# Mixture-of-experts block on one core: tokens picked for four experts at once from split rows, and expert outputs added to the residual by one-hot products

## Chip, cores and metric

One NeuronCore of a Trainium2 chip runs the whole two-layer block as one program. The metric is the device time of one execution in microseconds (us); lower is better. Engines are named as in the profile: PE (TensorE, matmuls), PEld (its weight loads), DVE (VectorE), ACT (ScalarE), POOL (GpSimd), SP (SyncE, which here only issues DMAs). PSUM is the memory that PE writes, 8 banks of 512 fp32 columns.

## What is computed

```
for layer in range(2):
    ...                                   # norm, three token mixers, merge, gated residual
    h  = modulate(rms_norm(x), ...)                       # (T, 1024), T = 512 in layer 0, 256 in layer 1
    g, top2 = route(h)                                    # one of 4 groups, two of its 8 experts
    w  = p_group * softmax over the two                   # (T, 2)
    for e in range(32):                                   # one SwiGLU expert, D 1024, width 512
        y_e = (silu(h @ w_gate[e]) * (h @ w_up[e])) @ w_down[e]
    x += gate * sum over the token's two experts of w * y_e
out = rms_norm(x[latent]) * g
```

Everything is fp32. Layer 0 carries 256 latent and 256 context tokens, layer 1 only the 256 latent ones. An expert's weights are 4.19 MB (gate and up) and 2.10 MB (down), so each layer streams 32 x 6.29 = 201.3 MB through its expert loop.

## The kernel before

The residual `xt` is kept transposed in SBUF: 8 chunks of 128 channels by 512 tokens. Each engine runs its own instruction stream, written by hand; semaphores order them. A layer is: norm, the mixers (PE products of weights that SP streams through the three slots of `ws`), merge and output product, second norm, routing, expert loop, combination.

**Split products.** In the mixers a product of fp32 matrices is made of three products of type fp32r: ACT rounds each operand to a high part, DVE leaves the low part (`round_weights`, `leave_weights`), and PE runs hi x hi, hi x lo, lo x hi (`product`, L457 to L459). The expert products (L709, L721), the picks (L700) and the transposes are plain fp32.

**Routing.** After the logits PE turns `ht` into token rows `hr` (4 tiles of 128 tokens by 1024), ACT copies them. DVE finds each token's two experts, its position within each (`place1`), the count `n_of` and the first row `start_of` of every expert in a sorted list, `dest` (the row of each token's output in that list) and the two weights `route_w`.

**Expert loop** (`Fori(0, 16)`, two experts per pass, slots s = 0, 1). Per expert PE runs: `gate_up` (8 chunks k by two halves j of the output width, the 64 token slots as stationary operand, 512 columns moving, the halves in the two 64-column halves of the array); the first half of `pick_x` for the next expert (one-hot product of `hr` with `pick`, 8 chunks by nt token tiles, 64 columns moving; nt is 4 in layer 0 and 2 in layer 1); `turn_h`; the second half of the pick; `down` (4 k by 2 halves). ACT does the silu, copies the 64 output rows out of PSUM and stores them to the DRAM tensor `y_rows` (`save_rows`). DVE multiplies silu by up (L1415), copies the turned rows (L1433) and the picked tokens (L1435) and sets the next `pick` (L1378). An expert with more than 64 tokens repeats the whole for its next 64 inside an `If` (the overflow block).

**Weights.** SP loads experts e and e+1 into two slots; gate/up of e+2 waits for `turn_h` of e, down of e+2 for `down` of e:

```
sp.wait_ge(g["hidt_done"].sem, NE * l + 2 * i + slot - 1)
load_expert(source, slot, range(4))
sp.wait_ge(down_done[slot].sem, 16 * l + i)
load_expert(source, slot, range(4, 6))
```

**Combination**, after the loop: ACT waits until every row store has landed; POOL gathers the two rows of each token by indirect DMA (L1545), ACT and DVE weight and add them (L1080, L1449), PE turns the tile back (L783), DVE adds it to `xt` (L1443), ACT squares (L1073), PE averages the squares (L773), and ACT's root (L839) opens the next norm.

## Time and profile before

| | |
|---|---|
| median of 3 runs | 2273.63 us (2273.55 to 2279.94) |
| the profiled execution | 2275.08 us |
| its span | 2273.3 us |
| PE busy | 2084.5 us, 92% |
| DVE / ACT / POOL busy | 647.3 / 514.7 / 155.0 us |
| mean granted PE clock | 0.956 of full speed |

The span is the time from the first to the last record of one execution, the time of the execution has 1.8 us more around it. Places in the program are given as us from the start of the span: expert loop of layer 0 from 667 to 1289, of layer 1 from 1717 to 2234.

### The profile page before, as it was taken

Reading aid. Unit: us, or ns where it says so; the run is one execution under the profiler, and the core shown is the slowest. Engines: PE = TensorE matmul, PEld = TensorE weight load, DVE = VectorE, ACT = ScalarE, POOL = GpSimd, SP = SyncE. Lnnn points to the kernel's source line nnn. Section 1 sums busy time; section 2 is a strip of 40 time slices with the busy share of each in tenths; the row PEclk is TensorE's granted clock in tenths of the full one; section 3 lists DMA queues with packets and bytes.
Section 4 is the critical chain, followed back from the end, with each engine's and each line's share of the span. In section 5 each row is a group of like instructions: output and inputs, shape, how many; then the busy total and the mean of one; then the engine's idle time right before and its main releaser. Section 6 shows DMA issues by size and latency. Waiting matters only on the chain.

```text
span 2273.3 us, 31445 instructions
## 1 busy us (share of the span) xinstructions
PE 2084.5 (92%) x11703; PEld 1329.6 (58%) x11704; DVE 647.3 (28%) x1392; ACT 514.7 (23%) x1028; POOL 155.0 (7%) x190
## 2 busy tenths in 40 slices
PE   5899999999979999999999769988988999999995
PEld 2666666678746555656566457766765444444443
DVE  1554354345341100101011166373341111111112
ACT  2444333432220000100000154343131001111111
POOL 0043030000000000000000105040000000000000
PEclk8899999999979999999999889988998999999997
DMA  6266565123258998956888424232458679999992
GB/s 216 96 222 190 199 204 185 52 74 95 73 223 359 367 366 365 367 209 257 340 351 358 177 67 122 60 115 66 139 196 345 284 323 421 420 421 420 421 421 108
DMA packets 95915, 551.01 MB, mean 242 GB/s; under 512 B 14034, under 2 KB 15010, under 8 KB 42596
## 3 DMA queue, kind: packets, MB, share of 16 engines
q1 hardware_dynamic: 83108, 526.89, 59.5%
q0 software_dynamic: 4224, 11.35, 1.8%
q10 hardware_dynamic: 8512, 11.81, 1.5%
q8 instruction: 47, 0.77, 0.1%
q14 instruction: 24, 0.20, 0.0%
HBM read 537.15 MB, written 12.85 MB: 242 GB/s over the span
## 4 chain that ended last, share of the span: by engine, by line
PE 75%; DMA 10%; DVE 6%; ACT 5%; issue 2%; SPq 1%; ACTq 0%; POOL 0%; DVEq 0%; POOLq 0%
PE ps L709 19%; PE ps L700 15%; PE ps L721 9%; PE ps L457 7%; PE ps L459 7%; PE ps L458 7%; DMA moe<-in_w_exp_gate_up_dram 6%; PE ps L575 3%; DMA ws<-in_w_in_dram 2%; PE ps L604 2%; PE ps L586 1%; PE ps L497 1%; ACT w_hi L856 1%; DVE w_lo L1132 1%; PE ps L715 1%
## 5 line engine op out<-in xcount | busy, mean ns | idle before, releaser
L709 PE MATMUL ps<-moe,arena 128*64 128x512 f32 x2176 | 486.9, 600 | 10.6 <-DMA moe<-in_w_exp_gate_up_dram 5.6
L700 PEld LDWEIGHTS ps<-arena 128*128 128x128 f32 x3360 | 395.9, 196 | 58.3 <-issue 54.2
L700 PE MATMUL ps<-arena 128*128 128x64 f32 x3360 | 407.3, 279 | 5.9 <-DVE arena L1383 4.4
L709 PEld LDWEIGHTS ps<-moe,arena 128*64 128x64 f32 x2176 | 159.3, 139 | 325.8 <-issue 311.8
L457 PE MATMUL ps<-ht_hi,w_hi 128*128 128x512 f32 (+1 forms) x736 | 268.4, 365 | 26.6 <-DVE ht_lo L1155 17.9
L458 PE MATMUL ps<-ht_lo,w_hi 128*128 128x512 f32 (+1 forms) x736 | 257.7, 350 | 0.0
L459 PE MATMUL ps<-ht_hi,w_lo 128*128 128x512 f32 (+1 forms) x736 | 257.6, 350 | 0.0
L721 PE MATMUL ps<-moe,arena 128*64 128x512 f32 x1088 | 248.5, 598 | 2.1 <-DVE arena L1427 2.1
L1132 DVE TENSOR_TENSOR w_lo<-ws,w_hi 128x1024 fp32r<-128x1024 f32 (+1 forms) x124 | 152.5, 1233 | 288.4 <-ACT w_hi L856 288.3
L1415 DVE TENSOR_TENSOR arena<-aux,ps 128x256 f32<-128x256 f32 x64 | 27.0, 422 | 686.3 <-ACT aux L1030 686.3
L457 PEld LDWEIGHTS ps<-ht_hi,w_hi 128*128 128x128 f32 x736 | 140.0, 190 | 79.9 <-issue 50.0
L856 ACT ACTIVATE w_hi<-ws 128x1024 fp32r<-128x1024 f32 (+1 forms) x124 | 127.5, 1028 | 244.4 <-PE ps L459 129.9
L1053 ACT ACTIVATE arena<-ps 128x512 f32<-128x512 f32 x64 | 38.2, 597 | 529.8 <-PE ps L721 529.8
L459 PEld LDWEIGHTS ps<-ht_hi,w_lo 128*128 128x128 f32 x736 | 140.3, 191 | 18.5
L458 PEld LDWEIGHTS ps<-ht_lo,w_hi 128*128 128x128 f32 x736 | 140.7, 191 | 15.6
L721 PEld LDWEIGHTS ps<-moe,arena 128*64 128x64 f32 x1088 | 72.0, 136 | 123.8 <-issue 116.5
L1545 POOL DMA_INDIRECT arena<-y_rows,dest x12 | 11.6, 966 | 1658.2 <-ACTq L1065 947.9
L1030 ACT ACT_TABLE_LOAD x32 | 41.1, 1283 | 241.7 <-PE ps L709 241.7
L575 PE MATMUL ps<-arena 64*128 64x512 f32 (+1 forms) x192 | 87.5, 579 | 0.0
L1435 DVE COPY arena<-ps 128x512 f32<-128x512 f32 x64 | 44.3, 692 | 140.9 <-PE ps L700 140.9
L1030 ACT ACTIVATE aux<-ps 128x256 f32<-128x256 f32 x64 | 24.6, 384 | 201.0 <-PE ps L709 200.6
L586 PE MATMUL ps<-ident,moe 128*128 128x128 f32 x320 | 47.3, 290 | 18.5 <-DVE moe L1250 18.3
(207 smaller groups left out, 1844.1 us busy)
## 6 DMA issues: line engine op xcount, KB each, us to landing
moe<-in_w_exp_gate_up_dram SPq DMA_DIRECT2D x256, 1024.0 KB, 10.6
moe<-in_w_exp_down_dram SPq DMA_DIRECT2D x128, 1024.0 KB, 11.7
moe<-in_w_mod_dram SPq DMA_DIRECT2D x32, 1536.0 KB, 7.8
ws<-in_w_in_dram SPq DMA_DIRECT2D x92, 512.0 KB, 3.5
y_rows<-arena ACTq DMA_DIRECT2D x164, 64.0 KB, 5.7
ws<-in_w_branch_dram SPq DMA_DIRECT2D x16, 512.0 KB, 3.6
ws<-in_w_out_dram SPq DMA_DIRECT2D x16, 512.0 KB, 3.4
aux<-in_rpb_a_dram POOLq DMA_DIRECT2D x64, 64.0 KB, 2.7
```

The costliest lines, as they stand in the source:

```text
L457: pe.matmul(ps[:, bank, 0:cols], w[:, k, :], a_hi, start=(i == 0), stop=False)
L458: pe.matmul(ps[:, bank, 0:cols], w[:, k, :], a_lo, start=False, stop=False)
L459: mm = pe.matmul(ps[:, bank, 0:cols], w_lo[:, slot, k, :], a_hi, start=False, stop=(k == rows[-1]))
L575: mm = pe.matmul(score_bank[:, qt, 0:n], q_of(kind)[rows, h // 2, q0 + qt * P:q0 + (qt + 1) * P], kt_of(kind, h)[:, keys], start=True, sto ...
L586: mm = pe.transpose(prob_bank[:, tile, qt * P:(qt + 1) * P], prob[h % 2][:, qt, tile * P:(tile + 1) * P], ident[:, :])
L604: mm = pe.matmul(pv_bank[HD * hh:HD * hh + HD, 0:SEQ], v_of(kind, 2 * pair + hh, tile + (4 - n)), prob_t[hh][:, tile, :], start=(tile == 0 ...
L700: mm = pe.matmul(ps[:, dst_bank, c * BLK:(c + 1) * BLK], hr[:, tile, c * P:(c + 1) * P], picks[:, tile, :], start=(tile == 0), stop=(tile ...
L709: mm = pe.matmul(ps[BLK * j:BLK * j + BLK, bank, :].rearrange("p (g n) -> p g n", g=2), xs[:, k, :], w[:, k, 512 * j:512 * j + 512].rearra ...
L721: mm = pe.matmul(ps[BLK * j:BLK * j + BLK, bank, :], src[:, k % 2, BLK * (k // 2):BLK * (k // 2) + BLK], w[:, k, 512 * j:512 * j + 512], s ...
L856: nc.scalar.activation(w_hi[:, i % 2, 0:m], ws[:, slot, 0:m, :], ACT.Copy) \
L1030: nc.scalar.activation(act_g[s], ps[:, 2 + s, 0:256], ACT.Silu).then_inc(g["silu_done"].sem, 1)
L1132: v.tensor_tensor(w_lo[:, ws_slots[item], 0:m], ws[:, ws_slots[item], 0:m, :], w_hi[:, i % 2, 0:m].bitcast(F32), ALU.subtract).then_inc(g[ ...
```

## The change

* `hr` is held as `hr_hi` and `hr_lo` (both fp32r, ACT and DVE). `pick4` is a one-hot matrix for four experts, so a pick product moves 256 columns, not 64; it runs twice, for high and low rows. Each expert's pass does a quarter of the next four experts' picks (two of eight channel chunks), and ACT copies them into one of two buffers `xg`.
* The output rows of an expert stay in SBUF, scaled by the slots' routing weights `wsl` and split into `y_hi` (ACT) and `y_lo` (DVE). The pick matrix `pick_b` (bf16, twice side by side so that both halves of 64 rows hold it) is turned by PE into `spread_b` (slots by tokens), and three bf16 parts of the weights give `wsl`. Once per pair of experts, inside the first expert's `gate_up`, four rounds of eight products y x spread (64 rows deep, the two output halves in the array's two row halves) put 8 chunks into banks 3, 5, 7, and DVE adds them to `xt`.
* Gone: `y_rows`, `start_of`, `dest`, the row stores, the gathers, the weighting and turning after the loop. In their place stand one last combination and the ordinary `squares`/`mean`.
* The loop body now holds eight experts: `Fori(0, 3)` and a written-out last pass. All experts use bank 2 for gate/up and bank 4 for down. The overflow block picks from split rows, and ends with its own four combination rounds.
* `y_hi`, `y_lo`, `spread_b` lie in the memory of `ws`, so SP waits for the last combination before it loads layer 1's first mixer weights. POOL clears them once per layer.
* Routing: DVE makes `hr_lo` (`low_rows`) ahead of the positions.

```diff
@@ SP
-                        sp.wait_ge(g["hidt_done"].sem, NE * l + 2 * i + slot - 1)
+                        sp.wait_ge(g["slots_done"].sem, NE * l + 2 * i + slot - 1)
                         load_expert(source, slot, range(4))
...
+                sp.wait_ge(g["comb_done"].sem, 4 * EVENTS * (l + 1))
@@ PE
-                def pick_x(dst_bank, picks, sem, chunks=range(KC)):
-
-                    for c in chunks:
-                        for tile in range(nt):
-                            mm = pe.matmul(ps[:, dst_bank, c * BLK:(c + 1) * BLK], hr[:, tile, c * P:(c + 1) * P], picks[:, tile, :],
-                                           start=(tile == 0), stop=(tile == nt - 1))
...
+                def pick_chunk(bank, half, c, picks, n):
+
+                    for tile in range(nt):
+                        for rows in (hr_hi, hr_lo):
+                            mm = pe.matmul(ps[:, bank, n * half:n * half + n], rows[:, tile, c * P:(c + 1) * P], picks[:, tile, :],
+                                           start=(tile == 0 and rows is hr_hi), stop=(tile == nt - 1 and rows is hr_lo))
...
+                def combine(bank_done, done, ready, slots, event=None):
+
+                    def turn(rnd):
+                        banks = [COMBINE_BANKS[(2 * rnd + j) % 3] for j in range(2)]
+                        if rnd == 0:
+                            ready()
+                        pe.wait_ge(bank_done.sem, event + max(0, 2 * rnd - 1) + 1)
+                        terms = [(part[s], s) for s in slots for part in (y_hi, y_lo)]
+                        for n, (y, s) in enumerate(terms):
+                            for j in range(2):
+                                half = slice(BLK * j, BLK * j + BLK)
+                                mm = pe.matmul(ps[:, banks[j], 0:w_all], y[half, rnd * P:(rnd + 1) * P], spread_b[s][half, 0:w_all],
+                                               start=(n == 0), stop=(n == len(terms) - 1))
+                        mm.then_inc(done.sem, 1)
...
+                        if between and k in (2, 4, 6, 7):
+                            between((2, 4, 6, 7).index(k))
...
+                def turn_slots(picks, weights, sem):
+
+                    for tile in range(nt):
+                        pe.matmul(ps[:, 6, tile * P:(tile + 1) * P], picks[:, tile, :], ident_b[:, :], start=True, stop=True)
+                    for tile in range(nt):
+                        mm = pe.matmul(ps[:, 1, 256:259], picks[:, tile, :], weights[:, tile, :], start=(tile == 0), stop=(tile == nt - 1))
@@ ACT
-                        act.wait_ge(y_copied[s].sem, mine + 2)
-                        act.wait_ge(g["yo_saved"].sem, act.snap(n_more, min_val=0, max_val=64) * 32 + 32)
-                        save_rows(ysb[s], row, y_saved[s], rows=HALF)
...
+                        act.wait_ge(g["slots_done"].sem, own + 1)
+                        nc.scalar.activation(spread_b[s][:, 0:w_all], ps[:, 6, 0:w_all], ACT.Copy).then_inc(g["slots_copied"].sem, 1)
...
+                        nc.scalar.activation(y_hi[s][:, :], ps[:, 4, :], ACT.Copy, scale=wsl[:, s:s + 1]).then_inc(g["y_hi_set"].sem, 1)
@@ DVE
+                def add_round(rnd, done, signal, at):
+                    dve.wait_ge(done.sem, at + rnd + 1)
+                    for j in range(2):
+                        c = 4 * j + rnd
+                        for st, cols in streams(l):
+                            ins = v.scalar_tensor_tensor(xt[:, c, cols], ps[:, COMBINE_BANKS[(2 * rnd + j) % 3], cols],
+                                                         modv[:, l, st, 5 * KC + c:5 * KC + c + 1], xt[:, c, cols], ALU.mult, ALU.add)
+                        ins.then_inc(signal.sem, 1)
+
+                def leave_y(s, scale, signal):
+                    v.scalar_tensor_tensor(y_lo[s][:, :], ps[:, 4, :], scale, y_hi[s][:, :].bitcast(F32), ALU.mult, ALU.subtract).then_inc(signal.sem, 1)
@@ POOL
-                        pool.indirect_dma_start(out=yg[tile % 2][k], out_offset=None, in_=y_rows[0:2 * w_all, :],
-                                                in_offset=bass.IndirectOffsetOnAxis(ap=dest[:, k, tile:tile + 1], axis=0)) \
```

**How the order of instructions moves.** First PE, the end of an even expert's pass in layer 0 before (`arena` holds rows, picks and hidden rows, `moe` the weights): the turned rows, the second half of the pick, `down`, then the next expert's `gate_up` and the first half of its pick.

```order
L715 MATMUL ps<-ident,arena 128x128 [waits hid_done0]
L715 MATMUL ps<-ident,arena 128x128
L700 MATMUL ps<-arena 128x64 x16
L721 MATMUL ps<-moe,arena 64x512 [waits y_copied0,hidt_copied]
L721 MATMUL ps<-moe,arena 64x512 x7
L709 MATMUL ps<-moe,arena 64x512 [waits gu_in1,xt_copied]
L709 MATMUL ps<-moe,arena 64x512 x15
```

The same place now, from the last quarter of the even expert's `gate_up` (L735) on: a combination round (L725) stands after it, and the loop's branch comes before the picks (L710, here four of eight rows) and the turned slots (L745, L747).

```order
L735 MATMUL ps<-moe,xg_57 64x512 x2
L725 MATMUL ps<-spread_b_59,y_hi_61 128x512 [waits comb_added]
L725 MATMUL ps<-spread_b_59,y_hi_61 128x512
L725 MATMUL ps<-spread_b_59,y_lo_63 128x512 x2
L725 MATMUL ps<-spread_b_60,y_hi_62 128x512 x2
L725 MATMUL ps<-spread_b_60,y_lo_64 128x512 x2
L710 MATMUL ps<-pick_55,hr_hi 128x256 [waits pick4_set]
L710 MATMUL ps<-pick_55,hr_lo 128x256
L745 MATMUL ps<-ident_b,arena 128x128 [waits wsl_set,pickb_set]
L747 MATMUL ps<-mrow,arena 128x3 x4
L752 MATMUL ps<-ident,arena 128x128 [waits hid_done]
L758 MATMUL ps<-moe,arena 64x512 [waits hidt_copied]
```

Per expert 32 pick products of 64 columns became 16 of 256, and each pair of experts got 32 combination products. Second DVE, an even expert of layer 0: three rounds of additions to `xt` (L1469) stand ahead of the silu product (L1484), and one behind it, ahead of the copy of the turned rows.

```order
L1469 SCALAR_TENSOR_TENSOR xt<-ps,modv,xt 128x256 [waits comb_done]
L1469 SCALAR_TENSOR_TENSOR xt<-ps,modv,xt 128x256 x3
L1465 REGISTER_ALU
L1484 TENSOR_TENSOR arena<-aux,ps 128x256 [waits silu_done]
L1469 SCALAR_TENSOR_TENSOR xt<-ps,modv,xt 128x256 [waits comb_done]
L1469 SCALAR_TENSOR_TENSOR xt<-ps,modv,xt 128x256 x3
```

Where DVE had only the silu product (L1415) before the copy of the turned rows (L1433), it now has 16 additions of 256 columns around it.

## Rows read from the trace of the kernel before

**Rows 1.** Page, the chain that ended last, shares by engine.

```profile
PE 75%; DMA 10%; DVE 6%; ACT 5%; issue 2%; SPq 1%; ACTq 0%; POOL 0%; DVEq 0%; POOLq 0%
```

**Rows 2.** Stretches (us, busy and instructions by engine, clock, DMA share, GB/s): both loops.

```profile
680.00:966.00 286.00, 286.00 (x1821) 171.44 (x1820) 29.93 (x64) 25.97 (x40) 0.00 (x0) 1.00 0.89 362
...
2036.00:2219.50 183.50, 176.09 (x986) 88.11 (x984) 20.83 (x48) 19.48 (x31) 0.00 (x0) 1.00 1.01 421
```

**Rows 3.** The chain (start, us, what), layer 0 loop, one expert.

```profile
687.88 6.87 PE ps L709 x32
694.75 3.72 PE ps L700 x32
698.46 0.23 PE ps L715 x2
698.69 3.52 PE ps L700 x32
702.21 3.58 PE ps L721 x16
```

**Rows 4.** The chain, layer 1 loop, DMA-bound stretch.

```profile
2036.33 7.09 PE ps L709 x32
...
2047.31 19.42 DMA moe<-in_w_exp_gate_up_dram
...
2066.87 3.19 PE ps L709 x13
```

**Rows 5.** Timeline of PE, fp32r products in layer 1's mixers and output product.

```profile
1347.16 0.39 PE L458 MATMUL ps<-ht_lo,w_hi 128*128 128x512 f32 x1
1347.39 0.40 PE L459 MATMUL ps<-ht_hi,w_lo 128*128 128x512 f32 x1
...
1684.85 0.28 PE L458 MATMUL ps<-mt_lo,w_hi 128*128 128x256 f32 x1
1684.97 0.28 PE L459 MATMUL ps<-mt_hi,w_lo 128*128 128x256 f32 x1
```

**Rows 6.** Groups by line and form (busy, mean ns, idle before).

```profile
L1053 ACT ACTIVATE arena<-ps 128x512 f32<-128x512 f32 x64 | 38.2, 597 | 529.8 <-PE ps L721 529.8
...
L1378 DVE TENSOR_TENSOR arena<-arena,slots 128x256 f32<-128x256 f32 x32 | 13.3, 415 | 0.0
...
L1155 DVE TENSOR_TENSOR ht_lo<-ht,ht_hi 128x512 fp32r<-128x512 f32 x16 | 11.1, 692 | 3.2 <-ACT ht_hi L869 3.1
...
L1301 DVE SCALAR_TENSOR_TENSOR xt<-ps,half_gate,xt 128x256 f32<-128x256 f32 x24 | 10.9, 480 | 30.9 <-PE ps L459 30.9
```

**Rows 7.** Page, DMA issues (count, KB each, us to landing), the row stores.

```profile
y_rows<-arena ACTq DMA_DIRECT2D x164, 64.0 KB, 5.7
```

**Rows 8.** Timeline of PE, layer 0: expert 17's picks, its block's end.

```profile
981.25 10.93 PE L700 MATMUL ps<-arena 128*128 128x64 f32 x96
...
1008.52 0.43 PE L715 MATMUL ps<-ident,arena 128*128 128x128 f32 x2 [1.24 <-issue]
```

**Rows 9.** The chain, layer 1: gate_up of expert 2 and of expert 3.

```profile
1747.99 6.89 PE ps L709 x32
...
1784.01 1.28 PE ps L709 x5
```

**Rows 10.** Timeline from layer 0's last product to the root.

```profile
1285.29 3.65 PE L721 MATMUL ps<-moe,arena 128*64 128x512 f32 x16
...
1325.84 0.69 ACT L839 ACTIVATE aux<-ps,eps 128x512 f32<-128x512 f32 x1 [2.19 <-PE ps L773]
```

**Rows 11.** Timeline, the same in layer 1.

```profile
2230.46 3.65 PE L721 MATMUL ps<-moe,arena 128*64 128x512 f32 x16
...
2260.31 0.47 ACT L839 ACTIVATE aux<-ps,eps 128x256 f32<-128x256 f32 x1 [3.07 <-PE ps L773]
```

**Rows 12.** Timeline, start of layer 0's loop.

```profile
652.68 13.92 PE L700 MATMUL ps<-arena 128*128 128x64 f32 x64 [2.23 <-DVE arena L1383]
...
667.46 2.83 PE L709 MATMUL ps<-moe,arena 128*64 128x512 f32 x6 [0.87 <-DVE arena L1410]
```

More of the change, by code:

```diff
@@ L789, in _ @@
-                for bank in (2, 3, 4, 5):
-                    claim(bank)
-                mean_tile(nt - 1)
-                free[6] = (g["rstd_sqrt"], after)
+                        more_units = not (last and q >= 4)
+                        if more_units:
+                            if q % 4 == 0:
+                                pe.wait_ge(g["pick4_set"].sem, 8 * l + 2 * i + q // 4 + 2)
+                            pick_chunk(0, 0, 2 * (q % 4), pick4, 4 * BLK)
+                        pe.wait_ge(g["pickb_set"].sem, own + 1)
@@ L793, in _ @@
+                for c in COMBINED:
+                    mean(*after, c)
+            pe.wait_ge(g["comb_added"].sem, 8 * EVENTS * DEPTH + 1)
             for tile in range(2):
@@ L825, in squares @@
                     act.wait_ge(g["prep"].sem, g["prep"].at("xt", KC - 1))
-                for c in range(KC):
+                order = chunk_order(l, which)
+                for at, c in enumerate(order):
                     if which == "n2":
@@ L1084, in _ @@
-                square_tile(nt - 1)
-                root(*after, nt - 1)
+                        act.wait_ge(g["slots_done"].sem, own + 1)
+                        nc.scalar.activation(spread_b[s][:, 0:w_all], ps[:, 6, 0:w_all], ACT.Copy).then_inc(g["slots_copied"].sem, 1)
+                        if not (last and q >= 4):
+                            act.wait_ge(g["unit_done"].sem, own + 5)
+                            nc.scalar.activation(xg[(q // 4 + 1) % 2][:, 2 * (q % 4):2 * (q % 4) + 2, :],
+                                                 ps[:, 0, :].rearrange("p (c n) -> p c n", c=2), ACT.Copy).then_inc(g["unit_copied"].sem, 1)
@@ L1394, in _ @@
+                set_pick4(0)
+                for n in range(6, 2 * nt):
+                    low_rows(n)
                 dve.wait_ge(g["r_exp_done"].sem, g["r_exp_done"].at(l, 1))
@@ new lines, in eight_experts @@
+                        if not (last and q == 7):
+                            if q == 7:
+                                set_weights(e + 1)
+                            set_pick(pick_b, e + 1, 0, g["pickb_set"])
+                        if q % 4 == 3 and not last:
+                            dve.wait_ge(g["unit_done"].sem, own + 5)
+                            set_pick4(e + 5)
+                        dve.wait_ge(g["y_hi_set"].sem, own + 1)
+                        leave_y(s, wsl[:, s:s + 1], g["y_lo_set"])
@@ L1455, in _ @@
+                with dve.Fori(0, 3) as i:
+                    eight_experts(i, False)
+                eight_experts(3, True)
+                for rnd in range(4):
+                    add_round(rnd, g["comb_done"], g["comb_added"], 4 * EVENTS * l + 64)
             reciprocal_rms(DEPTH - 1, "fin")
```

440 lines of the change are left out of this document (223 added, 217 removed).

## Prediction

> **What bounds the kernel now.** I first read the chain that ended last: PE carries 75% of it, DMA 10% [rows 1]. The table of stretches then splits the two expert loops, which are half of the run. In layer 0 PE is busy for all of 286 us at full clock while the DMA engines stand at 0.89 of their time and 362 GB/s; in layer 1 DMA is at 1.01 and 421 GB/s, which is its ceiling here [rows 2]. So the first loop is bound by PE, the second by the stream of expert weights.
>
> The chain shows the parts of one expert in layer 0: gate/up 6.87 us, half a pick 3.72, the turn 0.23, the other half 3.52, down 3.58, together 17.92 [rows 3]. The picks are 7.2 of these. In layer 1, with two token tiles instead of four, they are half as long, so PE needs 14.3; but two experts take 2066.87 - 2036.33 = 30.54 us, 15.27 each, and a 19.4 us transfer stands in the chain between them [rows 4]. After each loop comes a stretch with little PE work: from the end of the last down product to the root of the next norm 1325.84 - 1288.94 = 36.9 us in layer 0 [rows 10] and 2260.31 - 2234.11 = 26.2 us in layer 1 [rows 11].
>
> **The change, layer 0 loop, per pair of experts.** Before: 2 x 17.92 = 35.8 us. Now:
> - gate/up and down as before, 2 x (6.87 + 3.58) = 20.9, turns 0.5 [rows 3].
> - Picks: 16 products of 256 columns per expert, fp32r. Neighbouring fp32r products of 256 columns start 0.118 us apart, those of 512 columns 0.23 [rows 5]. 2 x 16 x 0.118 = 3.8, in place of 14.5.
> - Turned slots and slot weights: 8 small bf16 products per expert, no row has their form. They stream 4 x 128 and 4 x 3 columns; between 0.2 (the column rate of rows 5) and 0.9 (each priced as a 256-column product) I take 0.4, nearer the first because columns are few: 0.8 per pair.
> - Combination: 32 products of 512 columns. No row shows two products in different row halves side by side. The two column halves of gate/up do run side by side: 16 fp32 products take 6.87, that is 8 times 0.86, and 0.86 is four passes of 0.215 [rows 3]. I take the same for row halves: 16 x 0.23 = 3.7; the other end is 7.4.
> - Eight changes between array layouts. Down is 3.58 where half of gate/up is 3.43, so a change shows as 0.15 [rows 3]; 8 x 0.15 = 1.2. The Trainium skill (TensorEngine Tiling, Key Properties) says that a change of tiling mode drains the engine, which speaks against this interleaving. A product of 512 columns lasts 0.39 us though the next starts 0.23 behind it [rows 5], so a drain would show about 0.16, and the row agrees.
> - Waits. The rounds use banks 3, 5, 7 in turn, so round 1 waits for one of DVE's additions, 2 for three, 3 for five. An addition to a chunk is two instructions of 0.48 [rows 6], so about 1.0 per chunk, and a gate/up step between rounds is 0.86, twice where two steps stand between. The first two waits are covered. Behind round 3 the queue is tight: on DVE the silu product stands behind three rounds of additions and the copy of the turned rows behind the fourth, 1.9 us. I put 0.4 there, and 0.3 for the branch, which PE now meets right behind gate/up. Bounds 0 and 3.
>
> Sum 31.3, 15.7 per expert; 4.5 us per pair saved, 16 pairs: -72. The last four experts carry no picks (4 x 1.9): -8. I give 4 back for what the expert at the head of each eight may wait (table load, copies of picks): -76.
>
> ACT and DVE stay hidden in this loop: per pair DVE has 7.7 us of additions, 1.4 of low parts (0.69 each [rows 6]) and some 6 of copies and one-hots, 15 of 31; if PE did not cover them, the bound would still be PE.
>
> **Overflow blocks.** Two in layer 0, two in layer 1. One costs 1008.52 - 984.9 = 23.6 us now, where 984.9 is a third of the way into the 96 pick instructions [rows 8]; in layer 1 expert 2 takes 36.02 instead of 14.3, 21.7 more [rows 9]. The block gains: outputs scaled and split (0.60 + 0.69 + hand-overs, 1.45), then four rounds with nothing to run beside the additions: 16 x 0.48 = 7.7 in layer 0, 3.8 in layer 1, and 1 for the rounds. The picks there keep 64 columns; 64 fp32r products, between 0.03 each (a quarter of the 256-column product) and 0.114 (today's picks, 10.93 / 96 [rows 8]); I take no gain. With the later start +11 each in layer 0, +7 in layer 1: +22 and +14.
>
> **Start of the loops.** DVE makes the low rows ahead of the one-hots: six of 0.69 and four one-hots of 0.42 [rows 6] before PE's first pick, two more low rows before it may start. PE's prologue of 64 products is between 7.6 (full clock) and 14 (half clock), today 13.9 and then a copy [rows 12]: +4 in layer 0, +2 in layer 1.
>
> **Layer 1 loop.** PE would need 20.9 + 0.5 + 1.9 + 0.4 + 1.9 + 1.2 + 0.7 = 27.5 per pair, 13.7 per expert, below the weights' 15.27. The row stores leave the DMA engines: two of 64 KB per expert [rows 7], 0.13 MB beside 6.29. At the same 421 GB/s an expert costs 6.29 / 6.42 x 15.27 = 14.96; over 30 experts -9. The longer blocks hold both weight slots, so DMA idles for what they add. Sum: -9 + 14 + 2 = +7.
>
> **Behind the loops.** Now: split (1.45), four rounds and the additions, squares and means chunk by chunk behind them. A mean is one fp32 product of 512 columns, 0.86 at full and 1.7 at half clock; eight of them at half clock are 13.7 and set the pace. From down to root 16 in layer 0 and, at half the width, 9.5 in layer 1: -21 and -17. Layer 1's first mixer weights now start behind the last round; three loads of under 4 us each lie beside the additions, the means and the root: nothing, and at most 4 if that cover is gone. The removed sort on DVE was off the path.
>
> **Sum:** -76 + 22 + 4 + 7 - 21 - 17 = -81, from 2275.08 for the profiled execution to 2194. The median of the runs shown lies 1.5 below that execution: **2193 us**.
>
> **The rivals.**
> A, the forecast, 0.64: layer 0 bound by PE at some 15.7, layer 1 by DMA. Its own range is 2165 to 2225.
> B, the row halves run one after the other, 0.10. For it: no row shows them together, and they read and write different places than the column halves. Against: the column halves do overlap. Price 3.7 x 16 = 59 in layer 0 and some 5 in layer 1: 2257. The Trainium skill (TensorE: Matmul & The Clock Gate, Part 3) measures four row tiles at 3.07 times one, so not full overlap; carried over to two halves that estimate adds 18 us to the sum.
> C, slower than before, 0.06: rounds and additions alternate. If each round can start only when DVE has finished the one before, and DVE does nothing while PE computes, every even expert stands for 4 x 1.92 = 7.7 us in layer 0 and 3.8 in layer 1. That is +7 x 16 = 112 and, as layer 1 then passes the weights' pace, about +25: 2330. It decides from 81 / 16 = 5.1 us of waiting per pair on. Against it: three banks, and 1.7 us of gate/up between most rounds.
> D, layer 0 becomes DMA-bound too, 0.16: small waits vanish, 15.0 per expert (-22), and the blocks' picks run at their columns' rate (-15): 2156.
> E, layout changes cost more than 0.15, 0.04: at the 0.39 us that a whole product lasts [rows 5], eight of them cost 1.9 more per pair, +31 in layer 0: 2224. This is the drain of the Trainium skill's page named above (TensorEngine Tiling) at its worst.
>
> **How the numbers follow.** What this kernel's measurement tells from no change is 0.3%, 6.8 us, so faster means below 2266.8. A, D, E and most of B lie there: 0.64 + 0.16 + 0.04 + 0.07 = 0.91. Same is B's rest, 0.03. Slower is C, 0.06. The range 2148 to 2240 leaves out B's and C's middle and the edges of A and D.
>
> **What would show it.** Layer 0's loop near 568 us instead of 621.5, picks as 256-column products 0.12 apart, the two products of a combination step starting together, PE idle under 1 us in an even expert. In layer 1 15.0 us per expert with DMA still full. From the last down to the root about 16 and 9.5 us. I am wrong if combination products of a step start 0.2 us apart (B), if PE's waits are on DVE's `xt` (C), or if DMA waits appear in layer 0 (D).

## The result, and the profile after

The changed kernel takes 2298.72 us (median of 4 runs, 2292.02 to 2305.78) against 2273.59 for the kernel before (median of 4 runs too; the table above has the first three): 1.0105 times as long, interval 1.0075 to 1.0136. The forecast was 2193 us, in a range of 2148 to 2240. It is slower, by 25 us, and the forecast is off by 106. The profiled execution is the one of 2305.78 us, 30.6 us longer in span than that of before; the rows below are from it.

The page of the changed kernel first: the lines that answer to [rows 1], with the instruction queue, which the forecast did not weigh.

```profile
q8 instruction: 156, 2.56, 0.5%
...
PE 73%; DMA 9%; DVE 7%; issue 5%; ACT 5%; SPq 1%; DVEq 0%; ACTq 0%
```

The row stores are gone, and "issue" has grown from 2% to 5% of the chain: time in which TensorE waits for nothing that the profile shows. The queue that brings instructions moved 156 packets of 16 KB. In the kernel before it is this line:

```profile
q8 instruction: 47, 0.77, 0.1%
```

Next the table of stretches of the changed kernel (columns as in [rows 2]): layer 0's loop from its first gate/up to its last down, nearly two undisturbed pairs of experts within it, layer 1's loop, and in it the DMA-bound part.

```profile
667.33:1320.28 652.95, 575.52 (x3092) 267.15 (x3092) 204.69 (x490) 76.56 (x132) 0.00 (x0) 0.93 0.72 291
...
687.20:750.00 62.80, 61.90 (x359) 28.07 (x356) 23.53 (x56) 9.08 (x16) 0.00 (x0) 1.00 0.96 392
...
1734.53:2277.56 543.03, 490.55 (x2668) 203.86 (x2668) 134.78 (x332) 69.28 (x132) 0.00 (x0) 0.96 0.86 352
...
2003.00:2249.00 246.00, 225.35 (x1234) 90.22 (x1232) 62.17 (x153) 33.64 (x64) 0.00 (x0) 0.98 1.01 416
```

The same stretch of the kernel before:

```profile
667.46:1288.94 621.48, 614.41 (x3876) 366.28 (x3876) 63.78 (x136) 53.30 (x83) 0.00 (x0) 0.99 0.78 317
```

The two kernels enter this loop at the same moment. Within 687 to 750 us the new one does what was forecast: PE busy, full clock, and the weights run at 392 GB/s. Over the whole loop its PE is idle for 77 us where the old one's was for 7, the clock stands at 0.93, and DMA at 0.72. Less work, in more time.

The chain of the changed kernel for an undisturbed pair of experts in layer 0, the answer to [rows 3] (start, us, what):

```profile
687.20 6.87 PE ps L735 x32
694.07 1.14 PE ps L710 x8
695.21 0.24 PE ps L745 x4
695.45 0.08 PE ps L747 x4
...
696.76 3.58 PE ps L758 x16
700.35 2.58 PE ps L735 x12
702.92 1.12 PE ps L725 x7
704.04 1.87 PE ps L735 x8
705.91 1.12 PE ps L725 x8
...
712.20 0.46 issue
...
719.01 3.00 PE ps L735 x13
```

From 687.20 to 719.01 are 31.81 us for two experts, where 31.3 was forecast and 35.8 stood before. L710 are the wide picks, 1.14 + 0.95 = 2.1 us per expert in place of 7.2. A round of combination (L725) is 1.12 us for eight products of 512 columns; that is four pairs side by side, 0.92 at 0.23 each, and the change of layout ahead of them. The `gate_up` with its four rounds takes 12.0 us in all (700.18 to 712.20), where 6.87 and 3.7 leave 1.5 for the eight layout changes, 0.18 each; 1.2 was forecast.

Now a loop-back of the same loop, 84 us later. The timeline of PE (start, us, line, what, and in brackets the idle time before it and what ended it):

```profile
799.74 3.65 PE L758 MATMUL ps<-moe,arena 128*64 128x512 f32 x16
806.86 4.49 PE L735 MATMUL ps<-moe,xg 128*64 128x512 f32 x12 [3.47 <-issue]
```

The first three steps of the next gate/up take 4.49 us where the pair above has 2.58. The table of stretches tells why, and the last row of it shows the same in a block's picks (the last three columns are clock, DMA share, GB/s):

```profile
799.80:803.30 3.50, 3.50 (x17) 1.00 (x16) 1.62 (x5) 0.60 (x1) 0.00 (x0) 1.00 0.95 342
803.40:806.80 3.40, 0.00 (x0) 0.00 (x0) 0.75 (x1) 1.97 (x2) 0.00 (x0) 1.00 1.01 419
806.86:811.30 4.44, 4.44 (x14) 1.12 (x14) 0.00 (x0) 0.00 (x0) 0.00 (x0) 0.62 1.01 415
981.70:992.60 10.90, 10.90 (x54) 10.90 (x54) 0.00 (x0) 0.00 (x0) 0.00 (x0) 0.50 0.01 5
```

TensorE stands for 3.47 us with nothing to wait for, then works at a granted clock of 0.62, most of it at the lower level of 1.2 GHz. So a stop of 3.5 us costs 5.4. The weights stream at 419 GB/s throughout, and are not missing. The list of waits (line, releaser: us in all, times, longest) shows how often it happens from 667 to 1320 us:

```profile
PE ps L710 <- issue: 38.0, 20, 6.7
PE ps L745 <- issue: 9.0, 6, 2.7
PE ps L725 <- DVE xt L1469: 7.3, 7, 1.4
PE ps L735 <- issue: 6.4, 2, 3.5
```

In these lines TensorE stands 53 us by issue, with four more in lines not shown, where the kernel before has 2.6 in all. Not all of it has one cause: 17 of the 57 us stand inside or at the end of the two overflow blocks. The wait that rival C feared, on DVE's `xt`, is 7.3, and 5.8 of that stands in the blocks' rounds too.

Last the overflow block of expert 17, timeline of PE, the answer to [rows 8]:

```profile
970.48 7.04 PE L735 MATMUL ps<-moe,xg 128*64 128x512 f32 x32
980.22 0.30 PE L710 MATMUL ps<-pick_o,hr_hi 128*128 128x64 f32 x1 [2.71 <-DVE pick_o L1494]
980.35 0.28 PE L710 MATMUL ps<-pick_o,hr_lo 128*128 128x64 f32 x1
...
992.36 0.40 PE L710 MATMUL ps<-pick_o,hr_lo 128*128 128x64 f32 x1
...
993.54 9.66 PE L735 MATMUL ps<-moe,arena 128*64 128x512 f32 x32 [0.24 <-DVE arena L1496]
...
1010.54 0.50 PE L725 MATMUL ps<-spread_b,y_hi 64*128 64x512 f32 x2 [1.71 <-issue]
```

The 64 picks last 12.4 us: the first dozen stand 0.11 us apart, the rest 0.21, at a clock of 0.50, and gate/up behind them takes 9.66 instead of 7.04. After the fourth round PE stands another 6.64 us until 1024.36. From 977.52, where gate/up ends, that makes 46.8 us; with the half clock behind it, expert 17 lasts some 49 us longer than an expert without a block. Before it was 23.6, and 35 was forecast.

Between the layers the new kernel is faster, as was forecast. From the last down product to the root, the timeline has these rows for layer 0:

```profile
1316.63 3.65 PE L758 MATMUL ps<-moe,arena 128*64 128x512 f32 x16 [0.52 <-DVE arena L1512]
...
1339.38 0.69 ACT L903 ACTIVATE aux<-ps,eps 128x512 f32<-128x512 f32 x1 [0.59 <-PE ps L522]
```

19.1 us, against 36.9 before [rows 10] and 16 forecast. The timeline between them: 1.6 us for the split of the rows, 9.3 for the four rounds, three of which wait 0.97 each for DVE's additions, then 8.1 for the eight means, at a granted clock of 0.87. In layer 1 it is 2277.56 to 2290.98, 13.4, against 26.2 [rows 11] and 9.5. The account of the span: layer 0's loop +31.5, layer 1's +26.0 (543.03 against 517.06), the two stretches behind them -17.8 and -12.8, between root and next loop +3.9, the rest -0.2: +30.6 us. Single executions enter layer 0's loop anywhere from 667 to 678 us in this study, so parts of one or two us mean little.

### The profile page after: what moved, and what is told of

Read it like the earlier page. It is cut to its first block, busy times and chain, and to the rows that moved or that the text cites. A ratio compares the mean times of both kernels' runs of the same rounds, so it can differ in the third digit from the quotient of the medians.

```text
span 2303.9 us, 28909 instructions
## 1 busy us (share of the span) xinstructions
PE 2029.3 (88%) x10751; PEld 1170.4 (51%) x10752; DVE 862.5 (37%) x1919; ACT 554.8 (24%) x1138; POOL 145.5 (6%) x190
## 4 chain that ended last, share of the span: by engine, by line
PE 73%; DMA 9%; DVE 7%; issue 5%; ACT 5%; SPq 1%; DVEq 0%; ACTq 0%
PE ps L735 19%; PE ps L758 8%; PE ps L464 7%; PE ps L466 7%; PE ps L465 7%; PE ps L725 6%; PE ps L710 6%; DMA moe<-in_w_exp_gate_up_dram 6%; PE ps L583 3%; DMA ws<-in_w_in_dram 2%; PE ps L612 2%; PE ps L594 1%; PE ps L522 1%; ACT w_hi L920 1%; PE ps L504 1%
## 5 line engine op out<-in xcount | busy, mean ns | idle before, releaser
L735 PE MATMUL ps<-moe,xg 128*64 128x512 f32 x2048 | 480.7, 606 | 24.5 <-DMA moe<-in_w_exp_gate_up_dram 13.7
L735 PEld LDWEIGHTS ps<-moe,xg 128*64 128x64 f32 x2048 | 138.9, 138 | 292.2 <-issue 268.3
L1469 DVE SCALAR_TENSOR_TENSOR xt<-ps,modv,xt 128x256 f32<-128x256 f32 x456 | 192.6, 478 | 215.3 <-PE ps L725 210.2
L758 PE MATMUL ps<-moe,arena 128*64 128x512 f32 x1088 | 254.6, 609 | 10.5 <-DVE arena L1512 7.1
L710 PE MATMUL ps<-pick,hr_hi 128*128 128x256 f32 x384 | 119.1, 335 | 54.4 <-issue 45.5
L758 PEld LDWEIGHTS ps<-moe,arena 128*64 128x64 f32 x1088 | 73.5, 140 | 144.2 <-issue 122.9
L725 PE MATMUL ps<-spread_b,y_hi 64*128 64x512 f32 (+1 forms) x576 | 114.6, 404 | 25.5 <-DVE xt L1469 15.4
L725 PEld LDWEIGHTS ps<-spread_b,y_hi 64*128 64x128 f32 x576 | 55.8, 190 | 149.5 <-DVE xt L1469 101.6
L710 PEld LDWEIGHTS ps<-pick,hr_hi 128*128 128x128 f32 x384 | 81.7, 213 | 89.1 <-issue 89.1
L710 PE MATMUL ps<-pick,hr_lo 128*128 128x256 f32 x384 | 107.2, 304 | 4.8 <-issue 4.8
L1484 DVE TENSOR_TENSOR arena<-aux,ps 128x256 f32<-128x256 f32 x64 | 26.8, 419 | 193.4 <-ACT aux L1087 193.4
L725 PE MATMUL ps<-spread_b,y_lo 64*128 64x512 f32 (+1 forms) x576 | 98.2, 347 | 0.0
```

The costliest lines, as they stand in the source:

```text
L710: mm = pe.matmul(ps[:, bank, n * half:n * half + n], rows[:, tile, c * P:(c + 1) * P], picks[:, tile, :], start=(tile == 0 and rows is hr_ ...
L725: mm = pe.matmul(ps[:, banks[j], 0:w_all], y[half, rnd * P:(rnd + 1) * P], spread_b[s][half, 0:w_all], start=(n == 0), stop=(n == len(term ...
L735: mm = pe.matmul(ps[BLK * j:BLK * j + BLK, 2, :].rearrange("p (g n) -> p g n", g=2), xs(k), w[:, k, 512 * j:512 * j + 512].rearrange("p (g ...
L758: mm = pe.matmul(ps[BLK * j:BLK * j + BLK, 4, :], src[:, k % 2, BLK * (k // 2):BLK * (k // 2) + BLK], w[:, k, 512 * j:512 * j + 512], star ...
L1469: ins = v.scalar_tensor_tensor(xt[:, c, cols], ps[:, COMBINE_BANKS[(2 * rnd + j) % 3], cols], modv[:, l, st, 5 * KC + c:5 * KC + c + 1], x ...
```

## The experiments

Two theories. **Theory 1**: the loops' bodies have become too long for what TensorE keeps of its code at hand, so it stands at branches and at the loop's end, and comes back at half clock. **Theory 2**: it is the branch, which TensorE now meets directly behind gate/up and its rounds. Beside them stands the work in the blocks, which both kernels have. Each ratio below is to the kernel before as it ran beside that experiment, 2270.7 to 2272.1 us.

**The kernel before, with longer passes.** Nothing is changed but how many experts are written out in one pass of the loop.

```diff
-                with pe.Fori(0, NE // 2) as i:
-                    for s in range(2):
-                        e, done = 2 * i + s, NE * l + 2 * i + s
-                        mine = 16 * l + i
+                with pe.Fori(0, NE // 8) as i:
+                    for q in range(8):
+                        s = q % 2
+                        e, done = 8 * i + q, NE * l + 8 * i + q
+                        mine = 16 * l + 4 * i + q // 2
```

With 16 experts (the same edit, with 16):

> The kernel before with its expert loop written out 16 experts per pass instead of 2, nothing else changed. Theory 1 (the changed kernel's PE stalls, 'issue' of 2 to 7 us, are instruction fetch: its layer 0 pass holds 1420 matmuls, and what lies behind the first four or five experts of a pass must be fetched anew through DMA queues full of weights): this pass holds 1984 matmuls, so the same 2 to 4 us stalls appear in layer 0 although the order of the work is the old one, in 10 to 25 places; time 2273.6 + 25 to 70 us, and several times more bytes on the instruction queue (0.77 MB before). Theory 2 (the stalls come from the branch, which PE now meets directly behind gate/up): no stalls, time within 5 us of before.

Measured: 2304.94 us, 1.0146 times before (1.0102 to 1.0190), 146 packets on the instruction queue. The time is in Theory 1's range, the number of places is not: TensorE stands by issue for over 1.3 us, outside the blocks, in five places of the two layers, not in 10 to 25.

With 8 experts:

> The kernel before with 8 experts per pass: 992 matmuls in a pass of layer 0, about as many as the changed kernel's layer 1 pass (1040), which shows hardly any stall after its first pass. Theory 1: few stalls, 0 to 15 us over before. Theory 2: none, within 5 us.

Measured: 2306.64 us, 1.0153 (1.0104 to 1.0203), 153 packets. An old kernel with the old order of work, only written out further, loses over 30 us, more than the change did, and more than the 0 to 15 that Theory 1 had given it. TensorE stands by issue at each loop-back of layer 0 for 2.65 to 2.91 us, and the gate/up behind takes 8.5 to 8.8 us instead of 7.04. The first of them (timeline):

```profile
822.18 8.62 PE L709 MATMUL ps<-moe,arena 128*64 128x512 f32 x32 [2.65 <-issue]
```

Theory 2 falls as the sole cause.

**The changed kernel, 4 experts per pass.** The picks of the next four experts are gathered in a second buffer and moved over at the end of the pass.

```diff
-                with pe.Fori(0, 3) as i:
-                    eight_experts(i, False)
-                eight_experts(3, True)
+                with pe.Fori(0, 7) as i:
+                    four_experts(i, False)
+                four_experts(7, True)
```

> The changed kernel with a loop of 4 experts per pass (710 matmuls in layer 0): picks for the next four go to one buffer and are moved to the other at the end of a pass (a copy of 1 us each on ACT and DVE beside the down product). Theory 1: the stalls go (58 us in layer 0's loop, 19 in layer 1's) and with them DMA idles less: 2298.7 - 60 to - 80, that is 2220 to 2240 us, faster than before. Theory 2: every branch still stands behind gate/up, stalls stay, 2290 to 2305 us.

Measured: 2280.81 us, 1.0022 (1.0000 to 1.0044), 121 packets. The direction is right and the size missed: the stops inside a pass are gone save for one of 1.1 us and one of 2.7, but those at the loop's end stayed, six of 2.9 to 3.5 us in layer 0, and so did the blocks. The first of them (timeline):

```profile
739.97 4.49 PE L735 MATMUL ps<-moe,xg 128*64 128x512 f32 x12 [3.14 <-issue]
```

**The block taken out, with its code.** The branch stays, with one empty instruction inside (slots past 64 are left out).

```diff
                         with pe.If(n > BLK):
-                            with pe.Fori(1, nb) as b:
-                                ...
+                            pe.nop()
```

> The changed kernel, 8 experts per pass, with the overflow block's work left out of its If (a no-op stands there; tokens beyond the 64th of an expert are dropped), the count's load, the waits and the branch kept at their place: 530 matmuls per pass. Theory 1: no stall, and the four blocks (some 49 us each in layer 0, 31 in layer 1, with stalls) gone too: 2110 to 2150 us. Theory 2: stalls of 2 to 4 us at the branches stay: 2160 to 2200 us.

Measured: 2085.45 us, 0.9180 (0.9141 to 0.9218), 25 us below Theory 1's range, 62 packets, and stalls by issue from 667 to 1300 us of 3.4 us in all, none over 0.5. The block's code and its work together cost 213 us.

**The block's code left in, but never entered** (slots past 64 are left out), which tells the two apart:

```diff
-                        with pe.If(n > BLK):
+                        with pe.If(n > 8 * BLK - 1):
```

> The changed kernel with the overflow block's instructions all in place, but its condition set so that no expert enters it (the outputs of the slots past 64 are left out). The same work as in the kernel whose block has no instructions (2085.45 us), so every difference is the price of code that is only jumped over. Theory 1 (a large loop body is fetched late, and each late fetch also leaves TensorE at half clock behind it): TensorE's stalls by issue outside the blocks were some 50 us in the changed kernel, with as much again in half-clock stretches behind them, so 2140 to 2180 us, stalls at the loop's end and at the branches of experts 5 to 7, and over 130 packets on the instruction queue where the empty block had 62. Rival (the time is the work in the blocks, and code that is not run costs nothing): 2083 to 2095 us.

Measured: 2153.37 us, 0.9502 (0.9475 to 0.9529), and 156 packets. Code that is never run costs 67.9 us. It is that of TensorE, VectorE and ScalarE together; a run further down adds code to TensorE alone. In the profiled executions layer 0's loop takes 554.0 us against 502.5 without the code, layer 1's 485.6 against 474.1. The waits of this kernel from 667 to 1300 us:

```profile
PE ps L710 <- issue: 25.5, 19, 3.6
PE ps L745 <- issue: 8.9, 6, 2.6
PE ps L735 <- issue: 6.0, 2, 3.0
```

**The same of the kernel before.** Its stores must still write every row, so the place of a token is cut to the last slot and the block keeps one store of old rows (slots past 64 are left out).

```diff
-                        with pe.If(n > BLK):
+                        with pe.If(n > 8 * BLK - 1):
...
                     chain(v.tensor_reduce(pos_k[k], wide, AX, ALU.add))
+                    chain(v.tensor_scalar(pos_k[k], pos_k[k], float(BLK - 1), None, ALU.min))
```

> The kernel before, with TensorE, VectorE's and ScalarE's work of its overflow blocks never entered (the slots past 64 are left out: their places are cut to the last slot, and only the store of 64 old rows stays in the block, so that every row is written). Four blocks of 23.7, 23.6, some 20 and 18 us go: 2180 to 2195 us by both theories, since this kernel's loop shows no late fetch. It gives the change without its blocks: my forecast for the rest of the change was -81 minus the blocks' +36, so -117, against 2085.45 us that would be 2202; every us below that is what the forecast of the rest missed.

Measured: 2197.99 us, 0.9669 (0.9639 to 0.9699), 47 packets; 3 us above the expected range, and it holds four stores and their waits that the others have not. With it the 25 us come apart, by the medians. The runs of one kernel here lie 6 to 22 us apart, and by the intervals of the ratios each of the first three differences is good to some 10 us:

| | before | change | difference |
|---|---|---|---|
| the rest of the kernel | 2197.99 | 2085.45 | -112.5 |
| code that is jumped over | - | 67.9 | +67.9 |
| work in the four blocks | 75.6 | 145.4 | +69.8 |
| all | 2273.59 | 2298.72 | +25.1 |

**The block's picks turned round.** The one-hot slots become the stationary operand and the token rows move, 512 columns at a time.

```diff
-                                    for c in range(KC):
-                                        mm = pick_chunk(0, c, c, pick_o, BLK)
+                                    for j in range(2):
+                                        for tile in range(nt):
+                                            for rows in (hr_hi, hr_lo):
+                                                mm = pe.matmul(ps[0:BLK, 2 * j, :], pick_o[:, tile, :], rows[:, tile, 512 * j:512 * j + 512],
+                                                               start=(tile == 0 and rows is hr_hi), stop=(tile == nt - 1 and rows is hr_lo))
+                                        mm.then_inc(g["xro_done"].sem, 1)
+                                    for j in range(2):
+                                        pe.wait_ge(g["xro_copied"].sem, 2 * more + j + 1)
+                                        pe.nop(nofuse=True)
+                                        for c in range(4):
+                                            mm = pe.transpose(ps[:, 0, BLK * (4 * j + c):BLK * (4 * j + c) + BLK],
+                                                              xr_o[j][s][0:BLK, c * P:(c + 1) * P], ident[0:BLK, 0:BLK])
```

With 4 experts per pass:

> The changed kernel with 4 experts per pass, and in the block the picks turned round: the one-hot slots are the 64-column stationary operand and the token rows move, 512 columns each, so 16 products in layer 0 (8 in layer 1) in place of 64 (32) products of 64 columns, then two copies and 8 transposes of 64x128. Price: 16 x 0.23 = 3.7, a copy some 0.9, transposes some 1.2 and a wait, 6 to 7.5 us in place of 13.3 to 13.8 in layer 0, and 4.5 to 5.5 in place of 5.2 at full clock in layer 1. The block's code is also 42 products shorter. Theory 1: -13 from the picks and -5 to -15 from less code to fetch on 2280.81, so 2253 to 2263 us, which would be below the kernel before. Rival (what is saved on TensorE is lost in waits for VectorE's copies, or the block's end stall stays): 2268 to 2282 us.

Measured: 2212.86 us, 0.9735 (0.9709 to 0.9761), 63 packets. 40 us better than the best that was expected. Layer 0, the same block (timeline of PE):

```profile
948.61 0.45 PE L805 MATMUL ps<-hr_hi,pick_o 128*64 128x512 f32 x1 [2.70 <-DVE pick_o L1515]
...
954.59 7.09 PE L736 MATMUL ps<-moe,arena 128*64 128x512 f32 x32 [0.38 <-DVE arena L1520]
...
969.00 0.49 PE L726 MATMUL ps<-spread_b,y_hi 64*128 64x512 f32 x2 [1.71 <-issue]
...
982.83 0.57 PE L711 MATMUL ps<-pick,hr_hi 128*128 128x256 f32 x1 [6.60 <-issue]
```

From the first pick to gate/up 5.98 us in place of 13.3, and gate/up has full clock behind the same wait of 2.7: the granted clock is 1.00 over the wide picks and over gate/up, where it was 0.50 and 0.73. No stall at the loop's end is left, and the packets have fallen from 121 to 63: some 76 instructions less per expert brought the pass below a limit, which is placed further down.

With 8 experts per pass, as in the change:

> The same block with 8 experts per pass as in the changed kernel. Theory 1: -13 from the picks of layer 0 and -10 to -20 from less code to fetch per pass, which is longer here than with 4 experts: 2265 to 2276 us against 2298.72. Rival (code that is jumped over costs nothing): 2283 to 2287 us.

Measured: 2256.37 us, 0.9928 (0.9901 to 0.9956), 143 packets, so 42.4 below the changed kernel and 9 below the range of Theory 1. With 8 experts the pass is still too long, so these 42 are what the picks, their clock and a shorter jump give; with 4 experts they give 68, and the 26 more fit the loop's end: six stops and the slower gate/up behind each are gone.

**The block's inner loop ended after the blocks that there are.** It made 7 turns in layer 0 and 3 in layer 1, of which all but one found nothing to do (the lines below are TensorE's; the loops of the two other engines are changed alike).

```diff
-                            with pe.Fori(1, nb) as b:
-                                with pe.If(n > b * BLK):
+                            blocks = pe.snap((n + BLK - 1) >> 6, min_val=2, max_val=nb)
+                            with pe.Fori(1, blocks) as b:
```

> The kernel with 4 experts per pass and wide picks (2212.86 us), and the block's inner loop ending after the blocks that an expert has, in place of 7 turns (3 in layer 1) of which all but one find nothing to do. In that kernel TensorE stands still by issue for 6.60 and 6.71 us at the end of layer 0's blocks (7 turns, 6 of them empty) and 2.84 and 2.83 in layer 1's (3 turns, 2 empty): a line through both gives 0.95 us per empty turn. Theory 3 (the empty turns are the price, not a fetch): 2 x 5.7 + 2 x 1.9 = 15 us less, 2196 to 2202 us, the stalls near 1 us. Rival (it is the code behind the block that is fetched late): the stalls stay, 2210 to 2216 us.

Measured: 2207.40 us, 0.9693 (0.9664 to 0.9722). This is the fastest kernel of the study; the intervals of the two ratios overlap, so its lead over the one before it is likely, not sure. The stall at the end of the block:

```profile
983.50 0.57 PE L711 MATMUL ps<-pick,hr_hi 128*128 128x256 f32 x1 [2.11 <-DVE xt L1490]
```

It is now 2.11 us and ended by DVE's additions, where it was 6.60 and by issue; in layer 1 it went from 2.83 to 1.33. Six empty turns gone in layer 0 and two in layer 1 give the same 0.75 us each. So the empty turns were the price at this place, and I had first read those 6.6 us as a late fetch. The expectation forgot that the additions stand behind them: 4.5 and 1.5 us per block come free, 12 in all, not 15, and the medians show 5.5.

**The kernel before with 4 experts per pass**, to place the limit:

> The kernel before with 4 experts written out in a pass in place of 2; 8 and 16 had cost +34 and +32 us. TensorE's instructions in a pass of layer 0 (each product is two, its load and itself): 500 before, 1991 with 8, and 997 here. The passes that showed no late fetch have 500, 1143 and 1231, those that showed it 1543 and more. Theory 1 with a limit between 1231 and 1543: no difference, 2268 to 2278 us, and some 50 packets on the instruction queue. Rival (the loss grows with the pass's length from the start): +10 to +17, so 2282 to 2290 us.

Measured: 2302.43 us, 1.0137 (1.0100 to 1.0175), 116 packets. Both ranges are missed. The chain of this kernel and of the kernel before, at the same place:

```profile
739.66 3.00 PE ps L721 x14
742.67 2.69 issue
745.36 8.49 PE ps L709 x32
```

```profile
741.61 6.87 PE ps L709 x32
748.48 3.72 PE ps L700 x32
```

The new one stands at each of layer 0's seven loop-backs for 2.7 to 2.9 us, and nowhere in layer 1. What was wrong is my count of the pass. I had taken two instructions for each product in the program. But a plain float32 product of 512 columns is two products in the trace (16 in the program, `x32` in the row), each with its own load, and the 64-column picks split as well. Counted in the compiled code, TensorE's instructions in one pass of layer 0 are:

| kernel | instructions in a pass | packets | stands at the loop's end |
|---|---|---|---|
| before | 960 | 47 | no |
| change, block without code | 1560 | 62 | no |
| 4 experts, wide picks, no empty turns | 1648 | 63 | no |
| 4 experts, wide picks | 1664 | 63 | no |
| before, 4 experts | 1920 | 116 | yes |
| change, 4 experts | 1968 | 121 | yes |
| 4 experts, wide picks, padded | 1996 | 176 | yes |
| change, wide picks | 3321 | 143 | yes |
| before, 8 experts | 3840 | 153 | yes |
| change | 3929 | 156 | yes |
| before, 16 experts | 7680 | 146 | yes (it has one in each layer) |

The limit lies between 1664 and 1920. In the kernel before with 4 experts, layer 1's pass has 1408 and shows no such stop. The packets tell more when they are counted by stretch. From 640 to 1330 us, layer 0's loop and little else, the kernel before moves 5 and the one with 4 experts 71, in eight passes of 1920 instructions; the changed kernel moves 64 in four passes of 3929. An instruction has 64 bytes in the compiled code, so a packet of 16 KB holds 256, and these passes are 60 and 61 packets long in all. Above the limit it is thus not the end of a pass that is fetched anew but nearly all of it, every time, and TensorE stands for only a small part of that.

The Trainium skill (Runtime: NRT & Kernel Launch, Instruction fetch mechanics) gives TensorE room for 2048 instructions, refilled in blocks of 256, and says that a taken branch whose target is outside "the current 2-page window" forces a fetch. By the table the room can agree with the Trainium skill: 1920 instructions are 7.5 blocks of 256 and can touch nine, one more than fit, though no run here shows where the blocks lie. The two-page window does not: passes of 960 to 1664 instructions are four to seven blocks long, and jump back without a stop.

**The pass padded over the limit.** The kernel with 4 experts and wide picks, and after every expert's block:

```diff
+                        with pe.If(n > 8 * BLK - 1):
+                            for _ in range(40):
+                                pe.matmul(ps[:, 6, 0:P], pick_b[:, 0, :], ident_b[:, :], start=True, stop=True)
+                        pe.nop()
```

> The kernel with 4 experts per pass and wide picks (2212.86 us), and behind every expert's block a branch that is never entered, with 40 products in it: the same work, a pass of 1559 instructions on TensorE in place of 1231. Theory 1: over the limit, so late fetches at the loop's end of 3 to 3.5 us each with half-clock stretches behind them, and some 120 packets on the instruction queue: 2235 to 2265 us. Rival (code that is jumped over costs only its branch, 64 times some 0.1 us, and the gain of the wide picks was the picks'): 2213 to 2221 us.

Measured: 2344.03 us, 1.0344 (1.0295 to 1.0394), 176 packets. The same work with products that are never run, on TensorE alone, takes 131 us longer than without them, far beyond what I expected; in the profiled executions 45 of them are in layer 0's loop and 85 in layer 1's. Layer 0 has the stops of the forecast at its loop's end, and layer 1 has them in the middle of its passes too, as in this row:

```profile
2165.88 0.33 PE L753 MATMUL ps<-ident,arena 128*128 128x128 f32 x1 [1.55 <-issue]
...
2187.90 2.83 PE L736 MATMUL ps<-moe,xg 128*64 128x512 f32 x6 [3.41 <-issue]
```

Layer 1's pass has some 1800 instructions here. From 1650 us on this kernel moves 69 packets and the one without the padding 12, so a pass of 1800 is fetched anew as well, and the limit lies between 1664 and some 1800. Why it stops also within the pass stays open.

## Why the prediction was wrong

**The work per expert was right.** 31.81 us per pair against 31.3, with the wide picks at their rate, the row halves side by side, the layout changes at 0.18 each, DVE and ACT hidden. (The terms as listed give 31.6: the stated sum left out the 0.3 for the branch, which measured 0.46 behind the rounds and nothing that shows behind the other expert; over 16 pairs that is 5 us.) The loop without blocks and their code takes 502.5 us, against 575.7 for the kernel before without its blocks, 73 less where 76 was forecast. In sum the change without blocks and without their code gives -112.5 us; the forecast's -81 without its +36 for the blocks is -117. Rivals B, D and E fall with that. Of C nothing came true between the rounds of the pairs: one wait on `xt` of 1.4 us in layer 0's loop, behind a stop, in place of 112; the other 5.8 stand in the blocks.

**The step that failed first** is "0.3 for the branch, which PE now meets right behind gate/up", and with it that the loop's end was given no price at all. The order of instructions showed eight experts in a pass, each with a block of some hundred products that nearly always is jumped over. I counted what is run and not what is passed. It cost 67.9 us (the block's code left in but never entered, against the block without code). Of that 51.5 are in layer 0's loop, where TensorE stands 41 us by issue in place of 3 and runs at the lower clock behind the longer stops (4.4 us of it, worth 1.8, behind the one shown above), and 11.6 in layer 1's. The Trainium skill's page named above says that a taken branch can force such a fetch; I did not weigh it. Here it did so in passes above the limit only. The number that would have warned stands in the page of before, 47 packets on the instruction queue, beside a pass that was going to be four times as long.

**The second is "+11 each in layer 0, +7 in layer 1"** for the blocks. Of 36 us forecast, 69.8 came. The trace of expert 17 gives the parts: 12.4 us of picks where the bounds went from 2 to 7.3 (64 times 0.03 or 0.114) and 7.3, "no gain", was taken. 0.11 was indeed the price at full clock; at 0.50 it is 0.213, and the wait of 2.7 for the one-hots had no term; the clock fell 1.4 us behind its end, with the 64-column products running. Gate/up lost 2.6 by the same clock. The four rounds behind the block came as forecast, with 0.97 us of waiting in three of them. The block's end had stood before too, 1.24 us [rows 8], and became 6.64: the block now ends with a wait for the last additions, and the empty turns begin only behind it. That the old block's turns were mostly hidden behind its down product, 3.6 us of queued work, fits these numbers but was not tried.

**The stretches behind the loops** went the right way and were 3.2 and 4.2 us too hopeful. That they came so near is in part luck: the sum let the means, at half clock, set the pace with 13.7 us, which left 2.3 of its 16 for all else. They ran in 8.1, at a granted clock of 0.87, but only behind all four rounds, and the rounds took 9.3, since the last three wait for DVE's additions. **The start of layer 0's loop**, priced at +4, came at the same moment as before. **Layer 1** was forecast at the weights' pace, 14.96 us per expert. In both changed kernels with 4 experts per pass two experts take 29.9 us in the DMA-bound stretch, just that. In the changed kernel an expert takes 15.3 (214.2 us for fourteen, from 2035.43 on). TensorE waits for weights there and not by issue, and the DMA engines are full, but they bring 416 GB/s where the kernel with 4 experts and wide picks has 420. The two differ in the packets of the instruction queue, 26 from 2003 to 2249 us against 3 from 1950 to 2160; how so little traffic would cost 0.3 us per expert is not shown. Two rows of the kernel with wide picks and 4 experts (timeline of PE), each a gate/up ahead of which the weights were awaited:

```profile
1980.44 2.80 PE L736 MATMUL ps<-moe,xg 128*64 128x512 f32 x12 [1.53 <-DMA moe<-in_w_exp_gate_up_dram]
...
2010.37 2.79 PE L736 MATMUL ps<-moe,xg 128*64 128x512 f32 x12 [1.61 <-DMA moe<-in_w_exp_gate_up_dram]
```

**The range** ended at 2240 because each unknown was bounded within its own term, while the two costs that decided had no term. With 4 experts per pass and wide picks in the block, the change is worth what it was built for: 2212.86 us, and 2207.40 without the empty turns, 3.1% below the kernel before.

## What to carry to other kernels

When a loop with branches is written out further, count the machine instructions of one pass on TensorE, those that are jumped over too, and look at the packets of the instruction queue: while the pass fits they are few, and above the limit nearly the whole pass is fetched again each time, with a stop at the jump back wherever nothing else holds TensorE longer. Price a rarely entered block by itself, at the clock that its own waits leave, and with the empty turns of its loop. And when a stop shows as "issue", take the code away and leave it in unused before you name its cause; here these two runs split what the trace alone had mixed.

## What was not expected of the hardware

- Instructions that are never run cost 67.9 us in one kernel and 131 in another. The stops are 2.7 to 3.5 us each at the loop's end, and gate/up behind them takes 8.5 to 8.8 us instead of 7.04 in the old kernel written out further; in the changed kernel its first 4.4 us ran at a granted clock of 0.62.
- The limit on a pass lies between 1664 and some 1800 TensorE instructions, and it is sharp: 63 packets below it, 116 and more above. Above it nearly the whole pass is fetched again in every turn of the loop.
- After a wait of 2.7 us and 1.4 us of 64-column products the clock fell to 0.50; the same wait followed by 512-column products did not.
- An empty turn of the inner loop, a comparison and a jump over the block, costs some 0.75 us where nothing covers it (4.5 us less stall for six of them in layer 0, 1.5 for two in layer 1).
- Two fp32r products in different row halves of the array ran side by side: eight of 512 columns in 1.12 us, where one after the other they would take 1.84 at 0.23 each.
